# First attention of a two-block transformer kernel on one core: results taken in pairs and unscaled, two score pairs instead of three, two banks each for transposes and results

## The reference, cut to what matters

```python
s = einsum('bqhmd,bkhmd->bhmqk', qb, kk) * scale      # m = 0, 1: two score maps per head
p = softmax(s, axis=-1)
p = p[:, :, 0] - lam_full * p[:, :, 1]
o = einsum('bhqk,bkhe->bqhe', p, vv)
o = o * rsqrt(mean(o * o, axis=-1) + 1e-6) * subln_g * (1.0 - lam_init)
y = o.reshape(B, n, D_MODEL) @ wo
```

## Time and profile before

| what | value |
|---|---|
| three runs | 1104.08, 1106.25, 1109.86 us (median 1106.25) |
| the profiled execution: its own time | 1104.43 us |
| its span, first to last instruction | 1102.5 us |
| mean granted TensorE clock | 0.986 of full speed |
| first attention: S(1) to the small chain of the root | about 160.0 to 206.2 us |

### The profile page before, as it was taken

The page is one execution under the profiler, slowest core; times in us unless marked ns, Lnnn a source line. Parts: engine busy times, 40 slices in busy tenths (PEclk is TensorE's granted clock), DMA queues, the critical chain, the costliest instruction groups (busy, mean ns, idle before and its releaser), DMA issues.

```text
span 1102.5 us, 18256 instructions
## 1 busy us (share of the span) xinstructions
PE 1039.5 (94%) x7726; PEld 966.7 (88%) x7726; DVE 790.6 (72%) x1190; ACT 507.9 (46%) x700; POOL 0.7 (0%) x6
## 2 busy tenths in 40 slices
PE   4899999799999999999999999999999999989995
PEld 2679875699999999899989999999987998888984
DVE  3689759568787787888984655668746569876565
ACT  3623238444434334334544433454347566347562
POOL 0000000000000000000000000000000000000000
PEclk9899999899999999999999999999999999999998
DMA  9768541037998986666655666555653154345020
GB/s 365 277 217 311 186 172 39 1 122 275 311 309 293 313 289 229 208 229 233 209 188 195 213 218 222 189 153 176 207 191 125 39 182 152 120 156 193 1 78 38
DMA packets 116544, 210.14 MB, mean 191 GB/s; under 512 B 4250, under 2 KB 78192, under 8 KB 116464
## 3 DMA queue, kind: packets, MB, share of 16 engines
q1 hardware_dynamic: 115716, 206.81, 54.9%
q10 hardware_dynamic: 748, 2.18, 0.5%
HBM read 207.92 MB, written 1.05 MB: 190 GB/s over the span
## 4 chain that ended last, share of the span: by engine, by line
PE 72%; DVE 17%; ACT 4%; issue 4%; DMA 1%; SPq 1%; DVEq 0%; ACTq 0%
PE PS L1567 11%; PE PS L1568 11%; PE PS L1569 11%; PE PS L1652 7%; PE PS L1653 7%; PE PS L1671 7%; DVE low L976 4%; PE PS L1578 3%; PE PS L1975 2%; ACT high L579 2%; DVE ada_acc L955 2%; DMA ada_raw<-in_ada_w 1%; PE PS L1858 1%; PE PS L1690 1%; PE PS L1695 1%
## 5 line engine op out<-in xcount | busy, mean ns | idle before, releaser
L976 DVE TENSOR_TENSOR low<-raw,high 128x2048 fp32r<-128x2048 f32 (+2 forms) x147 | 328.1, 2234 | 163.3 <-ACT high L579 163.1
L579 ACT ACTIVATE high<-raw 128x2048 fp32r<-128x2048 f32 (+2 forms) x147 | 273.3, 1866 | 223.2 <-PE PS L1569 119.5
L1652 PE MATMUL PS<-hH,high 128*128 128x258 f32 x896 | 222.5, 285 | 5.4 <-DVE gated L1245 2.6
L1653 PE MATMUL PS<-hL,high 128*128 128x258 f32 x896 | 221.0, 284 | 0.0
L1652 PEld LDWEIGHTS PS<-hH,high 128*128 128x128 f32 x896 | 170.5, 190 | 7.2 <-issue 5.7
L1653 PEld LDWEIGHTS PS<-hL,high 128*128 128x128 f32 x896 | 169.4, 189 | 0.1
L1671 PE MATMUL PS<-hH,low 128*128 128x258 f32 x896 | 126.7, 284 | 2.2 <-DVE low L976 2.2
L1671 PEld LDWEIGHTS PS<-hH,low 128*128 128x128 f32 x896 | 116.2, 190 | 2.9 <-DVE low L976 2.9
L1567 PE MATMUL PS<-gH,high 128*128 128x256 f32 x352 | 98.5, 280 | 0.0
L1568 PE MATMUL PS<-gL,high 128*128 128x256 f32 x352 | 98.4, 280 | 0.0
L1569 PE MATMUL PS<-gH,low 128*128 128x256 f32 x352 | 98.2, 279 | 0.0
(11 more groups left out here) (315 smaller groups left out, 1941.7 us busy)
## 6 DMA issues: line engine op xcount, KB each, us to landing
raw<-in_ffn_w_in SPq DMA_DIRECT2D x44, 1024.0 KB, 6.3
ada_raw<-in_ada_w SPq DMA_DIRECT2D x82, 512.0 KB, 5.2
raw<-in_ffn_w_out SPq DMA_DIRECT2D x22, 1024.0 KB, 5.4
raw<-in_na_w_in SPq DMA_DIRECT2D x16, 1024.0 KB, 5.5
raw<-in_da_wqkv SPq DMA_DIRECT2D x12, 1024.0 KB, 8.1
raw<-in_sc_w_in SPq DMA_DIRECT2D x12, 1024.0 KB, 5.5
raw<-in_ple_w_gate SPq DMA_DIRECT2D x8, 1024.0 KB, 4.8
raw<-in_mla_w_in SPq DMA_DIRECT2D x7, 1024.0 KB, 5.2
```

The lines of the kernel that those rows point to most:

```text
L579: nc.scalar.activation(high[s][:, 0:width(u)], raw[s][:, 0:width(u)], ACT.Copy).then_inc(high_ready, 1)
L976: V_.tensor_tensor(low[s][:, 0:w], raw[s][:, 0:w], high[s][:, 0:w].bitcast(F), ALU.subtract).then_inc(low_dve, 1)
L1652: MM(PS[:, b + c, 0:SEQ + 2], high[s][w(j, c)], hH[:, j, 0:SEQ + 2], start=j == 0, stop=False)
L1653: MM(PS[:, b + c, 0:SEQ + 2], high[s][w(j, c)], hL[:, j, 0:SEQ + 2], start=False, stop=False)
```

## The change

- `SCORE_BANK` has two pairs, (0, 4). S(i+2) is issued in step i in place of S(i+3), and M(i+2) in place of M(i+3); S(2) and M(2) no longer stand ahead of the loop.
- The transposes use banks 6 and 2 in turn, the results banks 7 and 3 in turn.
- Two steps share a result bank, side by side. DVE takes them out in one copy of 128 x 256 at odd i, without dividing by the first sum; at even i it takes nothing. `o_taken` grows by 2 with each copy.
- P(i) takes the reciprocal of the second sum only, one column in place of two.
- Since the results are larger by the first sum s, the root takes ssq/128 + eps * s * s. One small instruction makes eps * s * s for all 16 columns ahead of the wait for the squares, one forms the argument, and `newton` is as before.
- On ACT the squares come later and behind the exponentials: Q(i-2) after E(i+2), and Q(14), Q(15) after the loop.

```diff
--- before.py
+++ after.py
@@ -50,7 +50,9 @@
     _at += _n
 NROWS = _at
 BROWS = 96
-SCORE_BANK = (0, 4, 2)
+SCORE_BANK = (0, 4)
+TURNED_BANK = (6, 2)
+SUM_BANK = (7, 3)
 GROUP_BANK = (6, 5, 4, 7)
 QK_BANK = (4, 5, 6, 0, 1, 2, 3, 4)
 HEAD_BANK = (0, 1, 2, 3)
@@ -659,7 +661,7 @@
             def da_exp(i):
                 seen.next(max_ready)
                 for m in range(2):
-                    ins = nc.scalar.activation(E[i % 3][:, m, :], bank(SCORE_BANK[i % 3] + m), ACT.Exp,
+                    ins = nc.scalar.activation(E[i % 3][:, m, :], bank(SCORE_BANK[i % 2] + m), ACT.Exp,
                                                bias=nmax[:, 2 * i + m:2 * i + m + 1], accum_out=esum[:, 2 * i + m:2 * i + m + 1])
                 ins.then_inc(exp_ready, 1)
 
@@ -675,7 +677,7 @@
 
             def da_pt(i):
                 seen.next(made_a)
-                nc.scalar.activation(PT[i % 2][:, :, :], bank(6).rearrange("p (k n) -> p k n", k=4), ACT.Copy).then_inc(probs_copied, 1)
+                nc.scalar.activation(PT[i % 2][:, :, :], bank(TURNED_BANK[i % 2]).rearrange("p (k n) -> p k n", k=4), ACT.Copy).then_inc(probs_copied, 1)
 
             def da_square(i):
 
@@ -687,10 +689,11 @@
             da_exp(1)
             for i in range(16):
                 da_pt(i)
-                if i >= 1:
-                    da_square(i - 1)
                 if i + 2 < 16:
                     da_exp(i + 2)
+                if i >= 2:
+                    da_square(i - 2)
+            da_square(14)
             da_square(15)
             at, _ = ROWS["da_subln_g"]
             outputs_high(oH, BY_HALF, cols[:, at:at + 1])
@@ -1146,12 +1149,11 @@
 
             def da_max(i):
                 seen.next(made_v)
-                V_.tensor_reduce(nmax[:, 2 * i:2 * i + 2], PS[:, SCORE_BANK[i % 3]:SCORE_BANK[i % 3] + 2, :], AX.X, ALU.max, negate=True).then_inc(max_ready, 1)
+                V_.tensor_reduce(nmax[:, 2 * i:2 * i + 2], PS[:, SCORE_BANK[i % 2]:SCORE_BANK[i % 2] + 2, :], AX.X, ALU.max, negate=True).then_inc(max_ready, 1)
 
             def da_probs(i):
                 seen.next(exp_ready)
-                link(V_.reciprocal(rsum[:, 2 * i:2 * i + 2], esum[:, 2 * i:2 * i + 2]))
-
+                link(V_.reciprocal(rsum[:, 2 * i + 1:2 * i + 2], esum[:, 2 * i + 1:2 * i + 2]))
                 link(V_.scalar_tensor_tensor(ratio[:, i % 2:i % 2 + 1], esum[:, 2 * i:2 * i + 1], rsum[:, 2 * i + 1:2 * i + 2], lam[:, 0:1],
                                              ALU.mult, ALU.mult))
                 V_.scalar_tensor_tensor(Pm[i % 2][:, :], E[i % 3][:, 1, :], ratio[:, i % 2:i % 2 + 1], E[i % 3][:, 0, :],
@@ -1162,19 +1164,26 @@
             da_probs(0)
             sections(first["da_v"] + 3)
             da_max(1)
-            da_max(2)
             for i in range(16):
                 t, h = divmod(i, 8)
                 if i + 1 < 16:
                     da_probs(i + 1)
-                if i + 3 < 16:
-                    da_max(i + 3)
-                seen.next(made_v)
-                V_.tensor_scalar(XN[:, t, h * P:(h + 1) * P], bank(7, P), rsum[:, 2 * i:2 * i + 1], None, ALU.mult).then_inc(o_taken, 1)
+                if i + 2 < 16:
+                    da_max(i + 2)
+                if i % 2:
+                    seen.next(made_v)
+                    V_.tensor_copy(XN[:, t, (h - 1) * P:(h + 1) * P], bank(SUM_BANK[i // 2 % 2], 2 * P)).then_inc(o_taken, 2)
+                else:
+                    seen.n[made_v.name] += 1
                 if i == 0:
                     split(first["da_v"] + 3 + RING)
+            at, _ = ROWS["da_subln_g"]
+            sums = esum[:, 0:32].rearrange("p (i m) -> p m i", m=2)[:, 0, :]
+            link(V_.scalar_tensor_tensor(rsum[:, 0:16], sums, EPS, sums, ALU.mult, ALU.mult))
             v.wait_ge(sq_ready, 16)
-            inverse_root(0, 16, P)
+            x = var[:, 0:16]
+            link(V_.scalar_tensor_tensor(x, ssq[:, 0:16], 1.0 / P, rsum[:, 0:16], ALU.mult, ALU.add))
+            newton(x, rst[:, 0:16], nwt[:, 0:16])
             for t, b in BY_HALF:
                 heads = XN[:, t, 512 * b:512 * b + 512].rearrange("p (h e) -> p h e", h=4)
                 k = 8 * t + 4 * b
@@ -1817,7 +1826,7 @@
                 behind(u)
             def da_scores(i):
                 t, h = divmod(i, 8)
-                b = SCORE_BANK[i % 3]
+                b = SCORE_BANK[i % 2]
                 claim(b, b + 1)
                 for m in range(2):
                     rs = slice(64 * m, 64 * m + 64)
@@ -1841,23 +1850,25 @@
                         pe.wait_ge(rope_done, 16)
                         da_scores(0)
 
-            for i in range(1, 3):
-                da_scores(i)
+            da_scores(1)
             pe.wait_ge(vz_copied, 8)
             for i in range(16):
                 t, h = divmod(i, 8)
                 seen.next(probs_ready)
-                claim(6)
-                transposes(6, [(k * P, P, Pm[i % 2][:, k * P:(k + 1) * P]) for k in range(4)]).then_inc(made_a, 1)
-                owed(probs_copied, 6)
-                if i + 3 < 16:
-                    da_scores(i + 3)
+                bt = TURNED_BANK[i % 2]
+                claim(bt)
+                transposes(bt, [(k * P, P, Pm[i % 2][:, k * P:(k + 1) * P]) for k in range(4)]).then_inc(made_a, 1)
+                owed(probs_copied, bt)
+                if i + 2 < 16:
+                    da_scores(i + 2)
                 seen.next(probs_copied)
-                claim(7)
+                bs = SUM_BANK[i // 2 % 2]
+                if i % 2 == 0:
+                    claim(bs)
                 for k in range(4):
-                    last = MM(bank(7, P), PT[i % 2][:, k, :], V[:, k, h * P:(h + 1) * P], start=k == 0, stop=k == 3)
+                    last = MM(PS[:, bs, i % 2 * P:(i % 2 + 1) * P], PT[i % 2][:, k, :], V[:, k, h * P:(h + 1) * P], start=k == 0, stop=k == 3)
                 last.then_inc(made_v, 1)
-                owed(o_taken, 7)
+                owed(o_taken, bs)
             output_groups(xn_ready, BY_HALF)
 
             def feature_out(u0, per_unit):
```

## The result

The changed kernel takes 1123.77 us (median of 4 runs, 1122.54 to 1127.12) against 1108.05 us of the kernel before (4 runs, 1104.08 to 1110.05). The ratio is 1.0162, with a 95% interval of 1.0140 to 1.0184: 1.6% slower, about 18 us. It isn't the quotient of the two medians, which is 1.0142, or 15.7 us. Predicted were 1124 us and a ratio of 1.0162.

A forecast was written before the change was run, and what follows sets the result against it. PE was taken to bound the kernel before, at 2.59 us per step; afterwards a 3.86 us ring over DVE and ACT. With start and end it loses 17.9 us, on the 1106.25 median 1124 us, range 1117 to 1129.

The forecast's parts named there:

- PE bounds before, at 2.59 us: First attention before the change: PE's transposes, scores and values set the pace, 2.59 us per step.
- The ring E, P, M: Attention loop: exponentials, combination and maxima wait for each other in one step per turn, 3.86 us per step.
- The start: Loop start: the weight unit's low part on DVE makes P(2) 0.59 us late; E(15) comes at 217.04.
- The end: Loop end: from E(15) at 217.04 to the root's first instruction at about 224.1, a loss of 17.9 us.
- The banks worth 0: Second banks for transposes and results: they remove two waits that the rows show not to be waits, gain 0.
- the pair copy and the eps term nearly 0: DVE and root: pair copies counted 0 except the last, 0.07 us longer; one reciprocal column and eps term together 0.05.
- Nothing behind catches up: From the root on: unchanged, no transfer catches up, 0 taken back, with 2 us either way.
- The clock stays at 1.00: PE in the loop: 67% busy with a 1.2 us pause each turn, granted clock expected to stay at 1.00.
- the second rival below: Second in the list: a ring through PE decides the loop's step, 3.05 us, about 1113 us in all; 6%.
- the third in its list: Rival that PE's clock falls to 1.2 GHz, making its 2.59 us per step 5.2, 1142 us; 5%.
- that PE hides it: Rival that PE's unchanged work still sets the loop's step: no change, at best 1105 us; 6%.
- The ring through PE: Rival that M needn't wait behind P, so a two-step ring of 6.1 us sets 3.05 a step, about 1113; 6%.

The follow-up runs named there:

- reordered kernel with the copy first: Changed kernel with scores ahead of transposes, values a step later, maxima ahead of combination, ACT's copy ahead of exponentials: 2.54 us per step, ratio 0.9990.
- kernel with all but the two pairs: The changed kernel with three score pairs again and one bank each for transposes and results: 2.59 us per step, ratio 0.9995.
- weight unit in step 13: The kernel before with the weight unit's low part moved from step 0 to step 13: S(1) to root 46.91 us, ratio 0.9989.
- reordered kernel without the copy first: Changed kernel with scores ahead of transposes, values a step later, maxima ahead of combination, exponentials ahead of ACT's copy: 2.76 us per step, ratio 1.0029.

## Why the prediction was right, step by step

- *PE bounds before, at 2.59 us*: shown by the doubled transposes, 0.43 us more per step there and none after the change.
- *The ring E, P, M of 1.48 + 1.12 + 1.26 = 3.86 us*: measured 3.86. Shown to come from the two score pairs alone, 17.36 of 17.83 us.
- *The start*: P(2) came 170.07 - 167.99 = 2.08 us after E(2), 0.60 later than the ring's 1.48, where 0.59 was predicted. From E(1) to E(15) it took 218.68 - 164.13 = 54.55 us, predicted 54.63.
- *The end*: from E(15) to the root 225.77 - 218.68 = 7.09 us, predicted 7.1. From the last copy to the root 1.27 in place of 0.82 us, of which the pair and the second square are the cause.
- *The banks worth 0, the pair copy and the eps term nearly 0*: shown, 0.03 and 0.24 us.
- *Nothing behind catches up*: root to end within 0.1 us of before. That it is so close is luck: over all the kernels here this time lies between 895.7 and 899.2 us, and the changed kernel with one bank each has 899.1. It goes with the granted clock from 900 us on, which is 0.97 on the mean in the executions with up to 897.7 us and 0.95 in those with 898.7 or more. So what is shown is that nothing is given back beyond some 3 us.
- *The clock stays at 1.00*: so it did, with pauses of 1.20 us in each step and one of 2.26 us ahead of V(14), at 218.70. The Trainium skill's page "TensorE: Matmul & The Clock Gate", section "A second HAM failure mode: psum-queue depth-cycling", had spoken for the other case; this loop, at 67% busy, doesn't show it. The prediction gives that case the time of "the second rival below"; the clock is the third in its list, with 1142 us. In the reordered kernel with the copy first the clock did fall, behind one pause of 1.84 us.
- *The rivals*: that PE hides it, with no change, is ruled out. The ring through PE at 3.05 us per step never showed: taking M from behind P closes another ring, of 4.15. Its price had been worked out on an order of DVE that can't be had without that ring, so its 6% was too much. Whether the other chances were well placed can't be told from one result.
- *Sizes*: ACT's wait for the maxima was 1.63 us in a step and not 1.5, as E holds ACT for 1.34 us (191.71 to 193.05) and not 1.44. The pair copy was to save DVE 2.1 us; in the kernel with all but the two pairs DVE's busy time from S(1) to the root is 38.58 us in place of 40.06, so 1.5 us less. The first enters the sum only at the end: V(14) came 2.28 us after E(15) where 2.37 was summed, and the last copy 1.26 us after V(15) where 1.20 was, which nearly cancel. The second doesn't enter it.
- *How much of the hit is luck*: the mechanism gave 17.9 us, and the stretch measures 17.83. That 1124 us and 1.0162 were met to the last digit is better than the measurement can tell. The 1124 stood on a median before of 1106.25, which four runs put at 1108.05, 1.8 us more, and the medians of the result lie 15.7 us apart, 2.2 us less than summed; the two nearly cancel. For the profiled execution the same sum gave 1122.3, and it took 1123.81, mainly since its S(1) came 1.73 us late.

## What to carry to other kernels

When a buffer is taken away from a software pipeline, don't ask whether the engines have time: write down, for every engine, its order of instructions, and follow each ring that the orders and the dependences close, with the number of steps that it spans. A step can't be shorter than the ring's sum divided by that number, nor than the work of the busiest engine; the largest of these sets it. The same buffers can be enough in another order, as here two score pairs at 2.54 us per step where they had cost 3.86, and a stray instruction in a queue is best put where nobody waits behind it, as here in step 14 and neither in step 0 nor in 13.

## What the runs showed of the hardware that I hadn't expected

The granted clock fell in two places behind pauses of PE that are shorter than others behind which it stayed. In the reordered kernel with the copy first it was 0.59 on the mean of 170.3 to 174.5 us, after PE had worked for 0.47 of 2.3 us with a pause of 1.84. With the weight unit in step 13, PE paused 1.48 us ahead of T(15) and again 0.69 us ahead of V(15), and the eight matmul records of V(15) took 2.08 us.

Against these stand three pauses with a clock of 1.00 in them and behind them: 1.72 us at 169.86 in the kernel before, 1.64 us in the same place of the reordered kernel without the copy first, and 2.26 us ahead of V(14) in the changed kernel, the longest of all.

```profile
...
169.86 0.66 PE L1578 MATMUL PS<-ident,gates 128*128 128x128 f32 x4 [1.72 <-DVE gates L1157]
...
```

So the length of the last pause alone doesn't decide. What of the time before it does wasn't tried.
